# Triangular inverses of two linear-attention layers: the transposed copy of small blocks by VectorE's 32x32 block transpose in place of a second TensorE product

## The reference, cut to what matters

```python
amat = jnp.where(strict, jnp.einsum('bhncd,bhnsd->bhncs', kb, k) * decay, 0.0)
rhs = jnp.concatenate([v * beta[..., None], kb * jnp.exp(gc)[..., None]], -1)
sol = lax.linalg.triangular_solve(amat, rhs, left_side=True, lower=True, unit_diagonal=True)
```

## Time and profile before

| | us |
|---|---|
| median of 3 runs | 2161.49 |
| the runs | 2158.42, 2161.49, 2161.50 |
| the profiled execution, its own time | 2158.44 |
| its span in the trace | 2156.6 |

### The profile page before, as it was taken

The page is one execution under the profiler, slowest core; times in us unless marked ns, Lnnn a source line. Parts: engine busy times, 40 slices in busy tenths (PEclk is TensorE's granted clock), DMA queues, the critical chain, the costliest instruction groups (busy, mean ns, idle before and its releaser), DMA issues.

```text
span 2156.6 us, 25033 instructions
## 1 busy us (share of the span) xinstructions
PE 2072.9 (96%) x10918; PEld 1472.8 (68%) x10918; DVE 1156.1 (54%) x1645; ACT 387.4 (18%) x780; POOL 10.7 (0%) x22
## 2 busy tenths in 40 slices
PE   8999898999999999999999989999999999989998
PEld 6887675796448469744884454988884457549973
DVE  2643666474530536653544583455555765646775
ACT  2413110100031410002112361211110011331110
POOL 0000000000000000000000000000000000000000
PEclk9999999999999999999999999999999999999999
DMA  5334686344444334534222101222224453113432
GB/s 195 118 118 172 244 338 253 136 182 166 168 159 161 117 125 164 195 136 148 91 93 102 40 1 39 79 79 79 78 83 165 190 186 131 69 66 130 171 146 114
DMA packets 22749, 292.69 MB, mean 136 GB/s; under 512 B 2752, under 2 KB 3008, under 8 KB 4848
## 3 DMA queue, kind: packets, MB, share of 16 engines
q1 hardware_dynamic: 20864, 280.67, 34.4%
q0 software_dynamic: 1776, 10.43, 1.3%
HBM read 290.03 MB, written 1.05 MB: 135 GB/s over the span
## 4 chain that ended last, share of the span: by engine, by line
PE 86%; DVE 8%; DMA 3%; ACT 1%; issue 0%; SPq 0%; DVEq 0%; ACTq 0%
PE bank L326 85%; DMA ring<-in_W 3%; DVE small L837 1%; PE bank L674 1%; DVE arena L858 1%; DVE arena L636 1%; DVE arena L685 0%; DVE arena L851 0%; PE bank L767 0%; DMA X<-in_x 0%; DVE arena L832 0%; DVE arena L1005 0%; DVE HT L2391 0%; ACT arena L683 0%; DVE arena L1517 0%
## 5 line engine op out<-in xcount | busy, mean ns | idle before, releaser
L326 PE MATMUL bank<-arena 128*128 128x128 f32 (+9 forms) x3856 | 679.1, 351 | 13.5 <-DVE arena L1598 3.7
L326 PEld LDWEIGHTS bank<-arena 128*128 128x128 f32 (+3 forms) x3856 | 475.2, 184 | 201.1 <-issue 157.8
L326 PE MATMUL bank<-HT,ring 128*128 128x128 f32 (+1 forms) x2672 | 461.4, 333 | 13.1 <-DMA ring<-in_W 4.7
L326 PEld LDWEIGHTS bank<-HT,ring 128*128 128x128 f32 x2672 | 410.4, 194 | 59.2 <-issue 21.0
L326 PE MATMUL bank<-ring,arena 128*128 128x512 f32 x690 | 302.9, 594 | 4.0 <-DMA ring<-in_W 4.0
L326 PEld LDWEIGHTS bank<-ring,arena 128*128 128x128 f32 x690 | 130.2, 190 | 165.1 <-issue 164.5
L326 PE MATMUL bank<-ring,HT 128*128 128x512 f32 (+2 forms) x512 | 199.1, 548 | 7.4 <-ACT HT L1950 2.9
L326 PE MATMUL bank<-arena,ring 128*128 128x128 f32 (+2 forms) x1046 | 172.5, 323 | 0.2 <-issue 0.2
L326 PEld LDWEIGHTS bank<-ring,HT 128*128 128x128 f32 x512 | 91.9, 196 | 110.0 <-issue 100.7
L683 ACT ACTIVATE arena<-bank 128x512 f32<-128x512 f32 (+2 forms) x127 | 69.4, 573 | 518.1 <-PE bank L326 487.2
L326 PEld LDWEIGHTS bank<-arena,ring 128*128 128x128 f32 (+1 forms) x1046 | 153.2, 191 | 13.0 <-issue 1.5
(11 more groups left out here) (297 smaller groups left out, 1523.5 us busy)
## 6 DMA issues: line engine op xcount, KB each, us to landing
ring<-in_W SPq DMA_DIRECT2D x125, 2048.0 KB, 7.8
ring<-in_W SPq DMA_DIRECT2D x6, 1536.0 KB, 9.4
ring<-in_W SPq DMA_DIRECT2D x4, 1024.0 KB, 9.6
arena<-in_rel POOLq DMA_DIRECT2D x1, 2048.0 KB, 10.0
arena<-in_rpb POOLq DMA_DIRECT2D x1, 2048.0 KB, 9.3
arena<-in_dft POOLq DMA_DIRECT2D x2, 640.0 KB, 6.6
X<-in_x SPq DMA_DIRECT2D x2, 512.0 KB, 5.9
X<-in_ctx POOLq DMA_DIRECT2D x1, 1024.0 KB, 5.1
```

What stands on the lines that cost most here:

```text
L326: return nc.tensor.matmul(out_, lhsT, rhs, start=start, stop=stop, skip_group_check=True)
```

## The change

In rounds 1 to 4 the products into XLXt go away, for both layers. VectorE adds XLX to `XI` alone, and then writes `XT` as the block transpose of `XI`: `nc.vector.transpose` on 128x512 transposes each 32x32 block where it stands, and up to blocks of 32 the tile has nothing outside the blocks on its diagonal. Round 5, whose blocks are 64 wide, is as before. The order on VectorE changes with it: the mask products of the next round now come first, for all groups, then the additions for all groups, then the transposes for all groups. TensorE waits for `XT` of a round ahead of its X L X; that wait is new. `dve_grow` no longer waits for XLXt in rounds 1 to 4.

```diff
         def pe_xlx(label, k, g, lx, XT):
             lab = f"{label} {k}.{g}"
             pe.wait_ge(scalar_done, at(f"read {lab} LX"))
+            if k > 1:
+                pe.wait_ge(vector_done, at(f"{lab} XT"))
             if k < 5:
                 ps = open_bank(lab + " XLX")
                 for i in range(4):
                     last = mm(ps[:, i * P:(i + 1) * P], XT[:, 4 * g + i, :], lx[g][:, i, :], True, True)
                 last.then_inc(tensor_done, pe.one())
                 pe.mark(lab + " XLX")
+                return
             ps = open_bank(lab + " XLXt")
...
         def dve_grow(label, k, g, XI, XT):
-            lab = f"{label} {k}.{g}"
-            dve.wait_ge(tensor_done, at(lab + " XLXt"))
-            for M_, n in ((XI, " XLX"), (XT, " XLXt"))[0 if k < 5 else 1:]:
-                ps = full(dve, lab + n)
-                tt(M_[:, 4 * g:4 * g + 4, :], M_[:, 4 * g:4 * g + 4, :], k4(ps[:, :]), ALU.add).then_inc(vector_done, dve.one())
-                dve.mark(f"read {lab}{n}")
-            dve.mark(f"{label} {k + 1}.{g} X")
+            n, M_ = (f"{label} {k}.{g} XLX", XI) if k < 5 else (f"{label} {k}.{g} XLXt", XT)
+            ps = full(dve, n)
+            tt(M_[:, 4 * g:4 * g + 4, :], M_[:, 4 * g:4 * g + 4, :], k4(ps[:, :]), ALU.add).then_inc(vector_done, dve.one())
+            dve.mark(f"read {n}", f"{label} {k + 1}.{g} X")
+
+        def dve_flip(label, k, g, XI, XT):
+
+            dve.wait_ge(vector_done, at(f"{label} {k + 1}.{g} X"))
+            src, dst = (v[:, 4 * g:4 * g + 4, :].rearrange("p a c -> p (a c)") for v in (XI, XT))
+            nc.vector.transpose(dst, src).then_inc(vector_done, dve.one())
+            dve.mark(f"{label} {k + 1}.{g} XT")
...
                 dve_ada(k - 1)
+                if k < 5:
+                    for g in range(4):
+                        dve_masked("rwkv", k + 1, g, MASKED1, LT1)
                 for g in range(4):
                     dve_grow("rwkv", k, g, XI1, XT1)
-                    if k < 5:
-                        dve_masked("rwkv", k + 1, g, MASKED1, LT1)
+                if k < 5:
+                    for g in range(4):
+                        dve_flip("rwkv", k, g, XI1, XT1)
...
                 dve_ada(9 + 2 * k)
+                if k < 5:
+                    for g in range(2):
+                        dve_masked("gdn", k + 1, g, MASKED2, LT2)
                 for g in range(2):
                     dve_grow("gdn", k, g, XI2, XT2)
-                    if k < 5:
-                        dve_masked("gdn", k + 1, g, MASKED2, LT2)
+                if k < 5:
+                    for g in range(2):
+                        dve_flip("gdn", k, g, XI2, XT2)
                 dve_ada(10 + 2 * k)
```

## The result

| | before, us | after, us |
|---|---|---|
| median | 2160.16 (4 runs) | 2144.46 (4 runs) |
| the runs | 2158.42 to 2161.50 | 2140.25, 2143.65, 2145.27, 2149.57 |
| the profiled execution, its own time | 2158.44 | 2149.57 |
| its span | 2156.6 | 2147.8 |

The ratio is 0.9929, with a 95% interval of 0.9905 to 0.9953: faster by 15.7 us. The profiled execution of after is the slowest of its four runs, so it has to be read by stretches. From the page, the lines that answer to the earlier trace rows: busy time by engine, and the chain by engine.

What follows compares the result with a forecast made beforehand. TensorE, busy 96% of the span, was taken as the bound; 10.9 - 0.3 + 4.8 = 15.4 us off 2158.44 gave 2143.0, plus half the difference between two run levels 2144.5; own range 2141 to 2148, 8 in 10 2137 to 2152.

Steps and rivals of the forecast that it cites:

- Rounds 1 to 3 of rwkv: Sixteen products fewer in each of three rounds, with VectorE's work covered by the half feature block: 10.9 us gained.
- The price of a transpose: VectorE's 128x512 block transpose taken at 0.69 us, hidden; a skill page's estimate was 1.24 us for four bfloat16 tiles.
- The end of round 4: In rwkv, 1.7 us gained less 2.0 us of low clock behind a 4.5 us TensorE idle time: -0.3 us.
- Gdn's rounds: Products of 7.3 us removed in four rounds, but weight loads queue from ada(18): 4.8 us gained, bounds 3 and 7.3.
- 1 us to spare: In gdn's round 4, VectorE's rwkv statistics end at about 319.5 us, before XLX of round 5 completes at 320.5.
- two levels: Whole-kernel times of the kernel before, 2158.4 or 2161.5 us; which the new median takes was left open.
- The half difference: Half the gap between 2158.4 and 2161.5 us, put on top of 2143.0 to give 2144.5 us.
- all of it counts: Rival: no low clock after round 4's idle time and loads keep up in gdn; 19.9 us gained, 2138.5 to 2141.5; 15%.
- More low clock: Rival: gdn's thinner rounds gain small waits, and two more clock falls cost 4 us: 2148.5 us; 15%.
- Slower than before: Rival: transposes at 3.35 us delay rwkv's round 4 and gdn's rounds: 2173 us; decides from about 2.5 us each; 6%.

Runs made afterwards that it cites:

- flips4: Changed kernel with every block transpose made four times, 2.8 us a group; median 2174.1 us, ratio 1.0064.
- flips2: Changed kernel with every block transpose made twice, 1.35 us a group in place of 0.60; median 2147.21 us, ratio 0.9940.
- after again: Second profiled execution of the changed kernel, no edit; the unedited kernel's new runs have median 2147.45 us, ratio 0.9931.
- half_loads: Changed kernel with the 13 ada weights from ada(11) to ada(23) loaded only in their first half, no TensorE instruction gone; median 2139.29 us.
- gdn_only: Changed kernel with the change kept for gdn alone, rwkv as before; median 2159.23 us, ratio 0.9991.
- before_early: Kernel before, second product kept, with VectorE's rwkv round 4 reordered: next masks and ada sum ahead, additions before the reciprocal; median 2158.31 us, ratio 0.9995.
- interleaved: Changed kernel with VectorE's old order, each addition followed by its group's mask product, transposes at the end; median 2140.59 us, ratio 0.9909.
- early_ada: Changed kernel with rwkv round 4's additions before the reciprocal and ada(20) moved into gdn's first chunk step; median 2134.55 us, ratio 0.9892.

## Why the prediction was right, point by point

The time came out at 2144.46 against 2144.5, which is closer than the steps behind it deserve.

- **Rounds 1 to 3 of rwkv**: 10.9 us forecast, 10.72 measured (A), in every kernel with the change for rwkv. The cover held: flips4 shows that even 2.8 us a transpose is hidden there.
- **The price of a transpose**: 0.69 us taken, 0.67 measured. In a row it is 0.60, as an addition. Of the two pages of the Trainium skill that the prediction names, the trace agrees with "Vector Engine (DVE) Microarchitecture Reference", section on the reshape front-end, by which it costs like a copy. The estimate of 1.24 us from the bfloat16 tile in the Trainium skill's "VectorE: DVE Perf Modes", section on the three transpose paths, is not what a row of 128x512 takes here. At 1.35 us, in flips2, A to E are no longer than in the changed kernel and F is 5.0 us longer.
- **The end of round 4**: -0.3 us forecast, -1.1 and -0.6 measured in after and after again (C). The idle time was 4.5 us in the forecast, 4.38 measured, and ended by the addition as said. The low clock took 6.35 - 3.73 = 2.6 us in after and 2.2 in after again, not 2.0; in half_loads, flips2 and flips4 it took 1.7, C was 13.59, and round 4 was 0.15 us longer than in before. The mechanism was right and the size within its bounds.
- **Gdn's rounds**: 4.8 us forecast, 3.0 and 4.3 measured (E), and half_loads shows the cause. In after again the waits begin ahead of ada(18), where I put them, and are 1.16, 1.00 and 0.99 us; in after they begin two blocks earlier, with 0.43 us ahead of ada(16), and four of about 1 us follow. Why they do in the one and not in the other isn't settled. The spacing of 5.0 us that I took was measured as 4.9. VectorE's "1 us to spare" held beside waiting loads only: in half_loads it is 0.8 us late.
- **B was missed altogether.** I had no term for the stretch from `bab` to XLX of round 4, and it gave 1.7 to 2.0 us in every kernel with the change for rwkv, and none in those without (1.9 in after). The weight of `bgate` was 7.66 us on its way in place of 8.61, and TensorE waited 0.69 us for it in place of 1.64 (2.05 in gdn_only). `bgate` itself ran 15.70 us, and in before longer:

```profile
189.63 16.60 PE L326 MATMUL bank<-ring,HT 128*128 128x512 f32 x32 [1.64 <-DMA ring<-in_W]
```

  The last 0.9 us is the shorter time at the low clock behind the shorter wait: 0.51 and 0.81 in the two stretches of 5 us from 188 in before, 0.73 and 0.93 in those from 180 in after. Why the load is faster is not settled, but it is no chance: it took 8.61, 8.78 and 9.02 us in before, before_early and gdn_only, and 7.55 to 7.78 in the other ten executions. The three have one packet of the instruction queue between its issue and its landing, and the ten have none. That was seen and not tried.
- **The clock between runs.** I put the forecast between two levels 3.1 us apart. There are no two levels: the 15 runs of before in the first group lie from 2157.3 to 2163.0 with values between, and the changed kernel's from 2140 to 2150 us, most of it by its granted clock. The half difference that I added happened to fit; the same kernel's next median, 2147.45, would have been 3 us off.

So the sum of the steps was 15.4 us, the stretches show A 10.7, B 1.9, C -1.1 to -0.6, D 0.4 to 1.0, E 3.0 to 4.3, which is 14.9 to 17.3. B and D, not forecast, made up for E and C, and D isn't owed to the change: before_early, which keeps all products, has 57.13 us there. What lies outside the stretches took 6 us back in both profiled executions, ahead of ada(0) and behind ada(21), and the forecast has no term for it. So the mechanisms in A, C and E were right, and that their sum met the median to 0.1 us is luck. The rival "all of it counts" fell with half_loads and the idle time. "More low clock" did not come where it was put: the clock is 1.00 from 272 to 330 us in after and after again. "Slower than before" is real as a mechanism, and flips2 and flips4 put its threshold between 1.35 and 2.8 us a transpose.

## What to carry to other kernels

- Work moved off the bound engine pays only where that engine has no other releaser close behind. Read the edges: here three places with products of the same kind removed gave all of their time (10.7 us), less than nothing, and about half (3.0 and 4.3 of 7.3 us), and each showed its next bound in the trace of before.
- When an edit reorders the engine that the bound engine waits for, put first what it waits for. Masks and additions moved ahead of a long instruction that nobody needed yet were worth 6 to 7 us in one stretch, nearly half as much as the whole change.
- A wait on TensorE costs its own length and can cost a low clock behind it: none behind 2.52 us in interleaved, 1.7 to 2.6 us behind 4.38.
- Where the clock differs from execution to execution, compare stretches between fixed instructions, and count what lies outside them too: flips2 lost 5 us in a stretch that its median doesn't show.

## What the runs showed of the hardware that I had not expected

- VectorE's 32x32 block transpose of 128x512 float32 takes 0.67 us alone and 0.60 in a row, the same as an addition, though it reads one operand.
- In flips4 TensorE's clock stayed at 1.2 GHz for 20 us behind a wait of 4.13 us, through 15 us without a gap on TensorE; in after the same kind of wait, 4.38 us, was followed by a mean of 0.62 and 0.70 in two stretches of 5 us, and in interleaved a wait of 2.52 us by 1.00 in both such stretches.
- The same kernel's runs differ by up to 10.6 us (early_ada), and time less span x (1 - clock) by 3 to 5, of which the rounding of the clock is 2.
